# Experts' weights of a two-block model moved, copied, used and handed back in 1 MB halves instead of 2 MB parts

## What is computed

```python
logits = (ht @ w_router + b_router).astype(jnp.float32)
top_vals, top_idx = lax.top_k(logits, TOP_K)          # TOP_K = 4 of N_EXPERTS = 32
gates = jax.nn.softmax(top_vals, axis=-1)
...
def expert_block(args):
    xblk, e = args
    gu = xblk @ w_gate_up[e] + b_gate_up[e]           # 1024 x 2048
    gate = jnp.minimum(gu[:, :D_EXPERT], SWIGLU_LIMIT)
    up = jnp.clip(gu[:, D_EXPERT:], -SWIGLU_LIMIT, SWIGLU_LIMIT)
    act = gate * jax.nn.sigmoid(SWIGLU_ALPHA * gate) * (up + 1)
    return act @ w_down[e] + b_down[e]                # 1024 x 1024
...
y = jnp.zeros((T + 1, D), h.dtype).at[row_tok].add(row_gate[:, None].astype(h.dtype) * yb)
```

## Time and profile before

| | |
|---|---|
| median of 3 runs | 1427.83 us |
| the profiled execution, its own time | 1420.85 us |
| its span, first to last instruction | 1419.1 us |
| granted TensorE clock, mean | 0.997 |
| TensorE matmul busy | 1362.6 us (96%) |
| GpSimd busy | 722.0 us (51%) |
| data moved | 480.79 MB, of which 402.7 MB are experts' weights |

### The profile page before, as it was taken

The page is one execution under the profiler, slowest core; times in us unless marked ns, Lnnn a source line. Parts: engine busy times, 40 slices in busy tenths (PEclk is TensorE's granted clock), DMA queues, the critical chain, the costliest instruction groups (busy, mean ns, idle before and its releaser), DMA issues.

```text
span 1419.1 us, 21427 instructions
## 1 busy us (share of the span) xinstructions
PE 1362.6 (96%) x7706; PEld 780.7 (55%) x7707; DVE 750.5 (53%) x1152; ACT 302.0 (21%) x454; POOL 722.0 (51%) x724
## 2 busy tenths in 40 slices
PE   8999999999999999999999999999989999999995
PEld 8899989999966744334334334334333333333332
DVE  7665788877655545445435545344344444433233
ACT  5645453344216201101001001001000000000001
POOL 3000024222154069888879888888888888500000
PEclk9999999999999999999999999999999999999998
DMA  9544355555557699999999999999999999999995
GB/s 320 167 144 135 119 186 171 177 182 194 184 199 269 270 361 428 428 428 428 428 413 429 429 427 427 429 428 428 427 428 429 428 429 429 429 428 428 428 427 214
DMA packets 77418, 480.79 MB, mean 339 GB/s; under 512 B 7019, under 2 KB 31272, under 8 KB 52808
## 3 DMA queue, kind: packets, MB, share of 16 engines
q1 hardware_dynamic: 74046, 477.45, 82.9%
q10 hardware_dynamic: 3338, 2.88, 0.6%
HBM read 479.26 MB, written 1.05 MB: 338 GB/s over the span
## 4 chain that ended last, share of the span: by engine, by line
PE 56%; DMA 33%; POOL 7%; DVE 2%; issue 1%; ACT 1%; POOLq 0%; SPq 0%; DVEq 0%; ACTq 0%
DMA stage<-in_w_gate_up 16%; PE bank L2362 13%; DMA stage<-in_w_down 7%; PE bank L2057 7%; DMA ring<-in_w_gate_up 7%; PE bank L1827 6%; PE bank L2438 6%; POOL ring_b L619 4%; PE bank L2085 4%; POOL ring L619 2%; DMA ring_b<-in_w_gate_up 2%; PE bank L1777 2%; PE bank L2348 2%; PE bank L1984 2%; PE bank L2022 2%; PE bank L1843 2%
## 5 line engine op out<-in xcount | busy, mean ns | idle before, releaser
L2362 PE MATMUL bank<-ring,x_T 128*64 128x512 f32 x1584 | 356.7, 596 | 24.0 <-POOL ring L619 16.7
L619 POOL COPY ring_b<-stage 128x1024 f32<-128x1024 f32 x252 | 260.9, 1079 | 45.3 <-DMA stage<-in_w_down 21.9
L2362 PEld LDWEIGHTS bank<-ring,x_T 128*64 128x64 f32 x1584 | 108.3, 137 | 251.4 <-issue 197.8
L2438 PE MATMUL bank<-ring_b,act_T 128*64 128x512 f32 x1056 | 233.9, 595 | 0.5 <-ACT act_T L961 0.5
L619 POOL COPY ring<-stage 128x1024 f32<-128x1024 f32 x192 | 198.5, 1078 | 38.8 <-DMA stage<-in_w_gate_up 30.4
L1647 DVE TENSOR_TENSOR h<-h,bank 128x512 f32<-128x512 f32 x128 | 82.2, 684 | 201.6 <-PE bank L2397 201.6
L2438 PEld LDWEIGHTS bank<-ring_b,act_T 128*64 128x64 f32 x1056 | 72.9, 137 | 144.2 <-issue 132.0
L2362 PE MATMUL bank<-ring_b,x_T 128*64 128x512 f32 x528 | 120.6, 598 | 7.6 <-POOL ring_b L619 5.3
L540 POOL TENSOR_TENSOR ff_lo<-ring,ff_hi 128x2048 fp32r<-128x2048 f32 x11 | 53.0, 4817 | 145.3 <-PE bank L2057 96.6
L955 ACT ACTIVATE sig<-bias_raw 128x512 f32<-128x512 f32 x33 | 20.8, 629 | 491.2 <-DVE bias_raw L1653 491.2
L619 POOL COPY ring<-stage_b 128x1024 f32<-128x1024 f32 x100 | 103.2, 1075 | 38.9 <-PE bank L2362 25.2
(11 more groups left out here) (474 smaller groups left out, 2110.9 us busy)
## 6 DMA issues: line engine op xcount, KB each, us to landing
stage<-in_w_gate_up SPq DMA_DIRECT2D x73, 2048.0 KB, 15.2
stage<-in_w_down SPq DMA_DIRECT2D x38, 2048.0 KB, 15.2
stage_b<-in_w_gate_up SPq DMA_DIRECT2D x25, 2048.0 KB, 14.8
ring<-in_w_gate_up SPq DMA_DIRECT2D x23, 2048.0 KB, 24.9
ring_b<-in_w_down SPq DMA_DIRECT2D x14, 2048.0 KB, 23.1
stage_b<-in_w_down SPq DMA_DIRECT2D x12, 2048.0 KB, 15.2
ring<-in_w_in SPq DMA_DIRECT2D x22, 1024.0 KB, 5.4
ring<-in_w_ffn_in SPq DMA_DIRECT2D x22, 1024.0 KB, 5.9
```

The source lines that it names most:

```text
L619: ins = pool.tensor_copy(pair_slot(g, k)[:, cols], stage_place(g, place)[:, cols])
L2362: ins = pe.matmul(banks[n][rows, :], t.x_T[:, c, :], job_slot(g, c)[:, c0:c0 + 512], start=False, stop=(c == GU - 1), skip_group_check=True)
L2438: ins = pe.matmul(banks[4][rows, :], t.act_T[:, k, SLOTS * (c // 2):SLOTS * (c // 2) + SLOTS], job_slot(g, GU + c)[:, c0:c0 + 512], start= ...
```

## The change

Every step of the way of an expert's part is done for each half of it.

- A part's 2 MB transfer becomes two of 1 MB (`load_half`, `stage_half`), each with its own semaphore (`in_place[k, i]`, `staged[place, i]`), 12 and 8 instead of 6 and 4. A partition's piece in memory is 8 KB instead of 16 KB (columns 2048 i to 2048 i + 2047 of the part).
- SP waits for each half's place and issues its transfer.
- GpSimd waits, for each half, for its landing and for the use of the old half, and copies it in two pieces of 1024 columns. The sizes of the copies stay.
- TensorE's `gate_up` takes i outside and n inside for pairs 0 to 2, so that the first half is used up at mid-part; for the last pair the order is (i, n) = (0, 0), (1, 0), (0, 1), (1, 1). It waits for each half. `down` waits at each c.
- `part_used` becomes `half_used`: `gu_used` counts 7 halves for each job, `gu_full` stands for the eighth, `d_used` counts as before but is waited for at each c.
- To make room for the new semaphores, the second set of scratch semaphores is dropped: the second block goes on counting in `filled`, `drained_act` and `drained_dve` (`Results(..., after=RESULTS)`); `place_free` is dropped, GpSimd increments `turn_begun`, for which nobody waits.

```diff
-def part_used(g, job, part):
-    if part < PAIRS - 1:
-        return g.s.gu_used, job * (PAIRS - 1) + (part + 1)
-    if part == PAIRS - 1:
+def half_used(g, job, part, i):
+    if part == PAIRS - 1 and i == 1:
         return g.s.gu_full, job * 2 + 2
-    return g.s.d_used, job * DN + 2 * (part - PAIRS) + 2
+    if part < PAIRS:
+        return g.s.gu_used, job * (GU - 1) + (2 * part + i + 1)
+    return g.s.d_used, job * DN + 2 * (part - PAIRS) + i + 1
+
+def half_of(place, i):
+    return place[:, 2 * D * i:2 * D * i + 2 * D]
...
+    def load_half(e, k, i):
+        sp.dma_start(half_of(pair_slot(g, k), i), half_of(part(e, k), i)).then_inc(s.in_place[k, i], 16)
+
     def load_part(e, k):
-        sp.dma_start(pair_slot(g, k), part(e, k)).then_inc(s.in_place[k], 16)
+        for i in range(2):
+            load_half(e, k, i)
...
     def next_part(e, last, k):
-        sp.wait_ge(*part_used(g, last, k))
-        load_part(e, k)
+        for i in range(2):
+            sp.wait_ge(*half_used(g, last, k, i))
+            load_half(e, k, i)
...
             for k in range(PARTS):
-                if k < PLACES:
-                    sp.wait_ge(s.in_place[k + PARTS - PLACES], m * 32 + 16 * (q + 2))
-                else:
-                    sp.wait_ge(s.in_place[k - PLACES], m * 32 + 16 * (q + 3))
-                load_stage(m * 2 + (q + 2), k, staged_at(q, k)[0])
+                for i in range(2):
+                    if k < PLACES:
+                        sp.wait_ge(s.in_place[k + PARTS - PLACES, i], m * 32 + 16 * (q + 2))
+                    else:
+                        sp.wait_ge(s.in_place[k - PLACES, i], m * 32 + 16 * (q + 3))
+                    stage_half(m * 2 + (q + 2), k, staged_at(q, k)[0], i)
...
     def put_in_place(last, k, place, landed):
-        pool.wait_ge(s.staged[place], landed)
-        pool.wait_ge(*part_used(g, last, k))
-        pool.sem_inc(s.place_free, 1)
-        for q in range(4):
-            cols = slice(1024 * q, 1024 * q + 1024)
-            ins = pool.tensor_copy(pair_slot(g, k)[:, cols], stage_place(g, place)[:, cols])
-        ins.then_inc(s.in_place[k], 16)
+        for i in range(2):
+            pool.wait_ge(s.staged[place, i], landed)
+            pool.wait_ge(*half_used(g, last, k, i))
+            pool.sem_inc(s.turn_begun, 1)
+            for q in (2 * i, 2 * i + 1):
+                cols = slice(D * q, D * q + D)
+                ins = pool.tensor_copy(pair_slot(g, k)[:, cols], stage_place(g, place)[:, cols])
+            ins.then_inc(s.in_place[k, i], 16)
...
-        pe.wait_ge(s.in_place[pair], e * 16 + 16)
-        for n in range(2):
-            for i in range(2):
-                c = 2 * pair + i
...
-            if pair == PAIRS - 1:
+        last = pair == PAIRS - 1
+        for i, n in ((0, 0), (1, 0), (0, 1), (1, 1)) if last else ((0, 0), (0, 1), (1, 0), (1, 1)):
+            if (i, n) in ((0, 0), (1, 0)):
+                pe.wait_ge(s.in_place[pair, i], e * 16 + 16)
+            c = 2 * pair + i
...
+            if last and i == 1:
                 ins.then_inc(s.gu_full, 1)
-        if pair < PAIRS - 1:
-            ins.then_inc(s.gu_used, 1)
+            elif n == 1:
+                ins.then_inc(s.gu_used, 1)
...
-            if c % 2 == 0:
-                pe.wait_ge(s.in_place[PAIRS + c // 2], e * 16 + 16)
+            pe.wait_ge(s.in_place[PAIRS + c // 2, c % 2], e * 16 + 16)
```

More of the change, by code:

```diff
@@ L106, with __init__ @@
 class Results:
-    def __init__(self, order, s, banks, first=0):
+    def __init__(self, order, s, banks, first=0, after=()):
         self.at = {name: n for n, (name, _) in enumerate(order)}
-        self.order, self.s, self.banks, self.first = order, s, banks, first
+        self.order, self.s, self.banks, self.first, self.after = order, s, banks, first, after
     def bank(self, name):
@@ L116, in filled @@
     def filled(self, name):
-        return self.s.filled, self.at[name] + 1
+        return self.s.filled, len(self.after) + self.at[name] + 1
     def drained(self, name):
@@ L123, in drained @@
         who = self.order[n][1]
-        return drained_sem(self.s, who), sum(w == who for _, w in self.order[: n + 1])
+        return drained_sem(self.s, who), sum(w == who for _, w in (*self.after, *self.order[: n + 1]))
     def room(self, name):
@@ L222, in __init__ @@
         self.nc, self.w, self.s, self.t, self.out, self.banks = nc, w, s, t, out, banks
-        self.r1, self.r2 = Results(RESULTS, s, banks), Results(RESULTS2, Filled2(s), banks, first=6)
+        self.r1, self.r2 = Results(RESULTS, s, banks), Results(RESULTS2, s, banks, first=6, after=RESULTS)
         self.first, self.second = front_chunks(w)
@@ L400, in part, with stage_half @@
         return gate_up[e, k] if k < PAIRS else down[e, k - PAIRS]
+    def load_half(e, k, i):
+        sp.dma_start(half_of(pair_slot(g, k), i), half_of(part(e, k), i)).then_inc(s.in_place[k, i], 16)
     def load_part(e, k):
-        sp.dma_start(pair_slot(g, k), part(e, k)).then_inc(s.in_place[k], 16)
+        for i in range(2):
+            load_half(e, k, i)
+    def stage_half(e, k, place, i):
+        sp.dma_start(half_of(stage_place(g, place), i), half_of(part(e, k), i)).then_inc(s.staged[place, i], 16)
     def load_stage(e, k, place):
-        sp.dma_start(stage_place(g, place), part(e, k)).then_inc(s.staged[place], 16)
+        for i in range(2):
+            stage_half(e, k, place, i)
     former = [("o", 3), ("g", 2), ("a", 1), ("o", 2), ("g", 1), ("o", 1)]
@@ L2152, in tensor_program @@
         ins = pe.matmul(bank[:, b * P:(b + 1) * P], t.ones[:], t.diag[:, b, :], start=True, stop=True)
-    ins.then_inc(s.filled2, 1)
+    ins.then_inc(s.filled, 1)
     for i in range(2):
-        u_block(i, 1).then_inc(s.filled2, 1)
+        u_block(i, 1).then_inc(s.filled, 1)
     pe.wait_ge(s.lat_ready, 2 * NB)
@@ L2228, in tensor_program @@
         pe.matmul(bank[:, 0:P], t.q_T[0:QK, h, 0:P], t.k_T[0:QK, h, 0:P], start=True, stop=True)
-        pe.matmul(bank[:, P:3 * P], t.q_T[0:QK, h, P:], t.k_T[0:QK, h, :], start=True, stop=True).then_inc(s.filled2, 1)
+        pe.matmul(bank[:, P:3 * P], t.q_T[0:QK, h, P:], t.k_T[0:QK, h, :], start=True, stop=True).then_inc(s.filled, 1)
     pe.wait_ge(*r2.drained("pm1"))
@@ L2309, in tensor_program @@
     for b in range(NB):
-        router(b, 1).then_inc(s.filled2, 1)
+        router(b, 1).then_inc(s.filled, 1)
     pe.wait_ge(s.bias_ready, 2)
@@ L2318, in tensor_program @@
     pe.matmul(bank[:, E:2 * E], t.ones[:], t.mask[:, 0, :], start=True, stop=False)
-    pe.matmul(bank[:, E:2 * E], t.before[:], t.mask[:, 1, :], start=False, stop=True).then_inc(s.filled2, 1)
+    pe.matmul(bank[:, E:2 * E], t.before[:], t.mask[:, 1, :], start=False, stop=True).then_inc(s.filled, 1)
     for b in range(NB):
@@ L2355, in gate_up @@
             pe.wait_ge(s.x_ready, nth(m, o, 2, 2))
-        pe.wait_ge(s.in_place[pair], e * 16 + 16)
-        for n in range(2):
-            for i in range(2):
-                c = 2 * pair + i
[L2360 to L2363, removed]
-            if pair == PAIRS - 1:
+        last = pair == PAIRS - 1
[3 more added lines that the diff above has]
+            c = 2 * pair + i
+            for half in range(2):
+                rows, c0 = slice(SLOTS * half, SLOTS * half + SLOTS), FE * n + 512 * half
+                ins = pe.matmul(banks[n][rows, :], t.x_T[:, c, :], job_slot(g, c)[:, c0:c0 + 512], start=False,
+                                stop=(c == GU - 1), skip_group_check=True)
+            if last and i == 1:
                 ins.then_inc(s.gu_full, 1)
-        if pair < PAIRS - 1:
-            ins.then_inc(s.gu_used, 1)
+            elif n == 1:
+                ins.then_inc(s.gu_used, 1)
     def turn_act(m, o):
@@ L2645, in __init__ @@
         self.out_ready = new("out_ready")
-        self.staged = [new(f"staged{n}") for n in range(PLACES)]
-        self.place_free = new("place_free")
-        self.in_place = [new(f"in_place{n}") for n in range(PARTS)]
+        self.staged = {(n, i): new(f"staged{n}{i}") for n in range(PLACES) for i in range(2)}
+        self.in_place = {(n, i): new(f"in_place{n}{i}") for n in range(PARTS) for i in range(2)}
         self.out_ready_act = new("out_ready_act")
```

16 lines of the change are left out of this document (5 added, 11 removed).

## The result

The changed kernel takes 1435.2 us (median of 18 runs, 1430.6 to 1438.8) against 1426.03 us for the kernel before (18 runs): 1.0063 times as long, 95% interval 1.0050 to 1.0076. It is slower by 9.2 us; 1434.7 us, or +6.9, was forecast.

What follows compares the result with a forecast made beforehand. The DMA stream, paced by its 16 engines, was taken as the bound, with a tail after it. Pace +13.6, rests -5.8 and tail -0.9 gave +6.9 us, from 1427.83 to 1434.7 us; range 1421 to 1439.

Steps and rivals of the forecast that it cites:

- The stream of transfers sets the end: From 546 us on: the DMA stream at 428 GB/s ends last, so the end is its end plus a tail.
- The cost of a packet, read from a line through 1 and 4 KB: DMA packets: 8.1 ns fixed each, 9 added packets a part, 73 ns or 1.5%, over 186 parts +13.6 us.
- the rests: Stops of the stream at 500 to 546 us and at 740; halved hand-backs were to save 5.8 us.
- 4.6 of the 5.5 us go.: Stream's rest from 500 to 546 us: halved hand-backs, first staging issue at about 507.3 instead of 511.1, remove 4.6 us.
- The rest at 740 goes: Stop from 740 to 748 us, at the expert with two jobs: first half back 3.8 us sooner, 1.2 us saved.
- The tail, -0.9 us: After the last gate and up part lands: only step (1, 0) is left before VectorE, 0.9 us less.
- The rest at nothing: SP's doubled issues, GpSimd's and TensorE's added waits, and the single set of scratch semaphores cost no time.
- A landing longer by about 1.5%: Sign of being right: a part's three-deep landing, 15.2 us before, grows by about 1.5%.
- The rival with half the fixed cost: DMA pace: 4.1 ns a packet costs 6.9 us, balanced by gains of 6.7; 425 GB/s, 1428.0 us; chance 0.18.
- the one with none: DMA pace: 428 GB/s is a shared ceiling, 8 KB pieces cost nothing, gains stand alone; 1421.1 us; chance 0.18.
- The rival in which the halves don't come back sooner: Hand-backs: first halves wait for landing or SP's turn, so the rests stay; +12.7 us, 1440.5 us; chance 0.08.
- the pace: Full-queue stream from 481 us on: smaller packets lower 428 GB/s to 421 to 423, +13.6 us.

Runs made afterwards that it cites:

- the 8 KB run: Kernel before with whole 2 MB transfers, hand-backs, copies and waits, but each partition's 16 KB read as two 8 KB pieces; 1434.88 us, ratio 1.0060.

## Why the prediction was right, point by point

- *The stream of transfers sets the end.* Right. Three kernels that differ in their pieces alone have 428, 421 and 410 GB/s, and the last gate and up part of the second and third lands 13.8 and 38.3 us later, counted from the direct issues (180 parts at the measured paces would be 14.4 and 39.8). TensorE has more idle time in each slower one.
- *The cost of a packet, read from a line through 1 and 4 KB.* Right in kind and in sign, and a little small. Beside the 612.4 ns at 16 KB the runs put 311.2 to 311.4 at 8 and 160.0 at 4: from 16 to 8 KB a part costs 8 added packets x 10.3 ns, the closing write taken in, where 9 at 8.1 had been reckoned; 0.082 us instead of 0.073. From its issue to the landing of the last gate and up part the changed kernel needs 902.9 us (503.24 to 1406.15) and the kernel before 892.7 (498.60 to 1391.33), 10.2 more. The 180 parts issued from there up to that one cost 180 x 0.082 = 14.8 us, and the rests give back 4.0. That leaves 0.6 us unexplained; two profiles of the kernel before differ by 0.35. The prediction had counted 186 parts: 13.6 us in all.
- *"4.6 of the 5.5 us go."* The term most off. The first issue came at 8.8 us, as forecast, but the window still rests 46 x (1 - 396/421) = 2.7 us, so 2.8 went. The sum had let a half that meets an empty queue run at full speed at once. It had GpSimd's copies at 2.0 us for a half, where those for part 3 took 2.5 (4.98 for four), and the 5.07 of the earlier trace rows had shown that already. `down` began 0.5 us late for the collision, which had no place in the sum. How the 1.8 us divide among these isn't shown. Part of what is left is no idle time either: in the changed kernel the engines moved 315, 307 and 348 GB/s from 526 to 532 us at shares of 0.96, 1.03 and 0.94, and why so little stays open.
- *The rest at 740 goes.* Right (421 GB/s), and for the reason given, which has two halves: the hand-back comes sooner and the stream is slower. Neither was enough where it was tried without the other: with copies by halves, but whole transfers at the old pace, 1.0 us stays, and with the slower pace and whole hand-backs 1.5. (Hand-backs by halves all through at the old pace were not tried.)
- *The tail, -0.9 us.* Right: from the landing to VectorE's first step 1.17 us instead of 2.02, so -0.85.
- *The rest at nothing.* Right. Doubled issues and waits don't show; TensorE's jobs keep their 26.2 us.
- *A landing longer by about 1.5%.* Wrong: a staging transfer now takes 17.5 us from issue to landing instead of 15.2. A half is behind more transfers than a part was: with seven halves on their way it would wait for 7 x 2.49 = 17.4 us, an estimate that fits. It costs nothing.

Together, from the same start: 14.8 - 4.0 - 0.85 = +9.95, less the 0.6 us left open = +9.35, and at a clock of 0.997 the runs differ by 9.3. The rival with half the fixed cost (425 GB/s) and the one with none (428) were both ruled out by the 421 GB/s of the 8 KB run. The rival in which the halves don't come back sooner was tried as a kernel of its own and is 2.5 to 3.7 us slower than the change.

The mechanism was right, and the size was a quarter short: +6.9 against +9.2, just under the interval of the measurement (7.1 to 10.8). The rests were taken 1.8 us too high and the pace 1.2 too low. That the forecast time, 1434.7 us, lies only 0.5 from the measured 1435.2 is luck in part: the median of three runs that it started from was 1.8 us above that of eighteen.

## What to carry to other kernels

Where a stream of transfers is the bound, look at the size of the piece that lies in one run in memory before making transfers finer: plot ns for each packet against its size from transfers that the trace already holds, and multiply the fixed part by the packets that the edit adds. Earlier hand-backs are worth only the rests of the stream, and a rest removed ahead of another one can come back there. Finer steps can pay at the ends of a pipeline (the tail gave 0.85 us), so they can be tried there alone; here that made the loss go away, but no gain clear of the noise came of it.

## What the runs showed of the hardware

- A packet from memory to SBUF in a full queue took 45.9 ns at 1 KB, 160.0 at 4, 311.2 at 8 and 612.4 at 16 KB: 37.6 ns for each KB and 8 to 10 ns fixed. The 429 to 432 GB/s with two thirds of the bytes in 32 KB pieces lie on the same line. The Trainium skill's 3 cycles for a packet (DMA: Bandwidth & Descriptors, section Why small descriptors are slow (HBM only)), 3.5 ns as an estimate with its 850 MHz, are well under what was measured; the measurement decides.
- Two closing writes for a part instead of one cost 2 to 3 ns beside 4981 (800 to 1200 us, and 850 to 1350).
- A VectorE step of 128x512 with two inputs took 1.18 us instead of 0.69 while GpSimd copied. Four of GpSimd's copies took 4.98 us beside VectorE's steps for the activation (5.07 in the kernel before), and 3.98 a few us earlier, when VectorE was mostly idle.
- TensorE's clock fell to 0.50 for some 10 us in one profiled execution and not in another of nearly the same program, in each case after the same gap near 458 us. Other profiles have a shorter fall elsewhere (0.60 from 484 to 488 us with 8 KB pieces, 0.74 from 444 to 448 with whole transfers). The runs of one kernel differ by up to 10 us with their mean clock, more than most edits here; what decides it stays open.
